# Reordering the columns of a normalized activation so that whole tiles can leave the meta columns out

## The reference, cut to what matters

```python
xn = rmsnorm(h, norm_mix)                       # 16 meta + 1024 prompt rows; 32 sample rows
z = xn @ w_in                                   # B, C, H (512 each), q, k, v (512 each), gate (512), a, beta
conv_out, new_a = causal_dwconv(z_C * z_H, buf_a, conv_a_w)      # 3 taps: reaches 2 rows back
y_a = z_B * conv_out
qkv, new_qkv = causal_dwconv(z_qkv, buf_qkv, conv_qkv_w)         # 4 taps
o, S = gated_delta_chunked(q, k, v, g, beta, state)              # recurrent over all rows, meta rows too
y_b = rmsnorm(o, gdn_norm) * silu(gate)
h = h + concat([y_a, y_b]) @ w_out
h = h + relu(rmsnorm(h) @ w_up)**2 @ w_down
y_prompt = rmsnorm(h, norm_final)[:, 16:]       # the meta rows are dropped
```

## Time and profile before

| | |
|---|---|
| Time, median of 3 runs | 1257.67 us (1257.44 to 1259.98) |
| Profiled execution, its own time | 1257.46 us |
| Its span, first to last instruction | 1255.7 us |
| PE busy | 1237.1 us (99%), 7950 matmuls |
| DVE, ACT, POOL busy | 801.7, 462.4, 646.7 us |
| PE idle from 0 to 43.33 us | 43.33 - 36.41 = 6.9 us |
| PE idle from 200 to 477 us | 277.00 - 276.21 = 0.8 us |
| granted PE clock, mean | 0.998 |

### The profile page before, as it was taken

How to read it: one execution, slowest core, us unless ns; L and a number is a source line. 1 busy time by engine, 2 the same in 40 slices (tenths; PEclk the granted TensorE clock), 3 DMA queues, 4 the chain that set the end, 5 groups by cost and what they waited for, 6 DMA issues and landing times.

```text
span 1255.7 us, 20503 instructions
## 1 busy us (share of the span) xinstructions
PE 1237.1 (99%) x7950; PEld 1090.9 (87%) x7950; DVE 801.7 (64%) x1283; ACT 462.4 (37%) x810; POOL 646.7 (52%) x503
## 2 busy tenths in 40 slices
PE   7999999999999999999999999999999999999997
PEld 6899999899999999998778888888887888878897
DVE  6465899535564766655987685565666667556456
ACT  6565654311222222224333333333434533333312
POOL 2332120112111212213889898888789989887811
PEclk9999999999999999999999999999999999999999
DMA  6132672843323322231145353444655442541003
GB/s 205 43 85 71 176 211 72 220 123 93 93 68 85 103 68 84 79 92 52 44 158 170 121 165 136 141 143 151 226 168 202 168 140 96 201 135 68 17 10 129
DMA packets 164706, 151.07 MB, mean 120 GB/s; under 512 B 21095, under 2 KB 141315, under 8 KB 161922
## 3 DMA queue, kind: packets, MB, share of 16 engines
q1 hardware_dynamic: 141634, 136.88, 34.4%
q10 hardware_dynamic: 22976, 12.88, 3.7%
HBM read 103.25 MB, written 46.49 MB: 119 GB/s over the span
## 4 chain that ended last, share of the span: by engine, by line
PE 95%; DVE 2%; POOL 1%; issue 1%; DMA 1%; ACT 1%; SPq 0%; POOLq 0%; DVEq 0%; ACTq 0%
PE banks L2328 15%; PE banks L2330 15%; PE banks L2331 15%; PE banks L1792 11%; PE banks L1794 11%; PE banks L1793 11%; PE banks L2359 1%; PE banks L2345 1%; PE banks L2441 1%; PE banks L2442 1%; PE banks L2443 1%; PE banks L2262 1%; PE banks L1978 1%; DMA w_raw<-in_w_in 1%; PE banks L1971 1%
## 5 line engine op out<-in xcount | busy, mean ns | idle before, releaser
L1792 PE MATMUL banks<-xn_high,w_high 128*128 128x384 f32 (+1 forms) x672 | 227.2, 338 | 1.0 <-DVE xn_low L2565 0.9
L1794 PE MATMUL banks<-xn_high,w_low 128*128 128x384 f32 (+1 forms) x672 | 218.9, 326 | 0.0
L1793 PE MATMUL banks<-xn_low,w_high 128*128 128x384 f32 (+1 forms) x672 | 218.8, 326 | 0.0
L1002 POOL TENSOR_TENSOR w_low<-w_raw,w_high 128x1024 fp32r<-128x1024 f32 x30 | 76.8, 2559 | 230.9 <-ACT w_high L1280 230.9
L3333 DVE TENSOR_TENSOR hT<-hT,banks 128x512 f32<-128x512 f32 x148 | 98.3, 684 | 109.2 <-PE banks L2331 108.4
L1792 PEld LDWEIGHTS banks<-xn_high,w_high 128*128 128x128 f32 x672 | 127.1, 189 | 6.8 <-issue 3.6
L2328 PE MATMUL banks<-op_high,set_high 128*128 128x512 f32 x336 | 131.6, 392 | 0.0
L2330 PE MATMUL banks<-op_low,set_high 128*128 128x512 f32 x336 | 130.8, 389 | 0.0
L2331 PE MATMUL banks<-op_high,set_low 128*128 128x512 f32 x336 | 130.7, 389 | 0.0
L1793 PEld LDWEIGHTS banks<-xn_low,w_high 128*128 128x128 f32 x672 | 127.4, 190 | 0.0
L1794 PEld LDWEIGHTS banks<-xn_high,w_low 128*128 128x128 f32 x672 | 127.0, 189 | 0.0
(11 more groups left out here) (419 smaller groups left out, 2839.9 us busy)
## 6 DMA issues: line engine op xcount, KB each, us to landing
op_raw<-ops_kept SPq DMA_DIRECT2D x21, 1024.0 KB, 5.0
w_up_raw<-in_w_up SPq DMA_DIRECT2D x16, 1024.0 KB, 6.5
w_raw<-in_w_in SPq DMA_DIRECT2D x28, 512.0 KB, 4.4
ops_kept<-u_rows SPq DMA_DIRECT2D x28, 512.0 KB, 2.7
ops_kept<-u_T SPq DMA_DIRECT2D x42, 256.0 KB, 2.4
w_down_half<-in_w_down SPq DMA_DIRECT2D x3, 2048.0 KB, 9.0
w_down<-in_w_down SPq DMA_DIRECT2D x24, 256.0 KB, 4.2
w_raw<-in_w_out SPq DMA_DIRECT2D x8, 512.0 KB, 3.8
```

Of the source, the lines that this page charges most:

```text
L1002: pool.tensor_tensor(w_l[n % 2][:, :, :], w_raw[n % 2][:, :, :], w_h[n % 2][:, :, :].bitcast(F32), ALU.subtract).then_inc(w_low, 1)
L1792: pe.matmul(bank[:, 0:w], w_h[n % 2][:, k, :], hi[:, c0:c0 + w], start=(k == first), stop=False)
L1793: pe.matmul(bank[:, 0:w], w_h[n % 2][:, k, :], lo[:, c0:c0 + w], start=False, stop=False)
L1794: ins = pe.matmul(bank[:, 0:w], w_l[n % 2][:, k, :], hi[:, c0:c0 + w], start=False, stop=(k == last))
```

## The change

The columns of the normalized x (`xn_high`, `xn_low`) are laid out as meta, prompt, samples; the groups become 272, 384 and 416 columns wide. Everything that is made from them (q, k, v, C, H, B, `abT`) keeps its old layout, so each eviction of the last group is split in a main piece and a piece of 32 sample columns, and the first group's is a single piece. Tiles of gate and B skip the first 16 columns of group 0 and tiles of C and H the first 14, in the matmuls and in the evictions. The gate's rows in DRAM have no meta columns any more. The samples of token tile 0 are transposed with group 2 instead of group 0, as a fourth piece of each k-slice. `idle_products` is written in terms of `GROUPS[0][1]`, so its width goes from 208 to 240 columns.

```diff
-GROUPS = [(0, C0 + 2 * P), (C0 + 2 * P, 3 * P), (C0 + 5 * P, 3 * P)]
+GROUPS = [(0, META + 2 * P), (META + 2 * P, 3 * P), (META + 5 * P, 3 * P + NS)]
...
-        gate_d = scratch("gate_kept_rows", [NH, P, TOK])
+        gate_d = scratch("gate_kept_rows", [NH, P, KEPT])
...
+        def unused(n, g):
+
+            return {"gate": META, "B": META, "C": META - 2, "H": META - 2}.get(IN_TILES[n][0], 0) if g == 0 else 0
+
+        def group_tiles(g):
+
+            pieces = [(0, slice(NS, C0))] if g == 0 else []
+            pieces += [(t, slice(0, P)) for t in GTILES[g] if t]
+            return pieces + ([(0, slice(0, NS))] if g == 2 else [])
+
+        def main_cols(g, skip=0):
+
+            c0, w = GROUPS[g]
+            w -= NS if g == 2 else 0
+            return slice(skip, w), slice(NS + c0 + skip, NS + c0 + w)
+
+        SAMPLE_COLS = slice(3 * P, 3 * P + NS)
+
+        def feature_cols(g, skip=0):
+
+            return [main_cols(g, skip)] + ([(SAMPLE_COLS, slice(0, NS))] if g == 2 else [])
+
+        def without_meta(cols):
+            return slice(cols.start - META, cols.stop - META) if cols.start >= C0 else cols
...
                     act.wait_ge(acc_done, 3 * n + g + 1)
-                    if g == 0:
+                    made, kept = main_cols(g)
+                    act.activation(zb[:, 59 - NS + kept.start:59 - NS + kept.stop], bank[:, made], ACT.Copy)
+                    if g == 2:
                         act.activation(zb[:, 0:56].rearrange("p (b r) -> p b r", r=7)[:, :, 3:7],
-                                       bank[:, 0:NS].rearrange("p (b r) -> p b r", r=LSEQ), ACT.Copy)
-                        act.activation(zb[:, 59:59 + w - NS], bank[:, NS:w], ACT.Copy)
-                    else:
-                        act.activation(zb[:, 59 + c0 - NS:59 + c0 - NS + w], bank[:, 0:w], ACT.Copy)
-                    act.activation(dst[:, c0:c0 + w], bank[:, 0:w], ACT.Copy, scale=now).then_inc(acc_read_act, 1)
+                                       bank[:, SAMPLE_COLS].rearrange("p (b r) -> p b r", r=LSEQ), ACT.Copy)
+                    for made, kept in parts:
+                        ins = act.activation(dst[:, kept], bank[:, made], ACT.Copy, scale=now)
+                    ins.then_inc(acc_read_act, 1)
...
-                    act.activation(z[0][:, c0:c0 + w], bank[:, 0:w], ACT.Copy).then_inc(acc_read_act, 1)
+                    for made, kept in parts:
+                        ins = act.activation(z[0][:, kept], bank[:, made], ACT.Copy)
+                    ins.then_inc(acc_read_act, 1)
...
                 act.wait_ge(acc_read_dve, dve_reads_to(n) + g + 1)
-                act.activation(ya_h[:, i, c0:c0 + w], z[1][:, c0:c0 + w], ACT.Copy).then_inc(ya_high_s, 1)
+                parts = feature_cols(g, unused(n, g))
+                for _, kept in parts:
+                    cols = without_meta(kept)
+                    ins = act.activation(ya_h[:, i, cols], z[1][:, cols], ACT.Copy)
+                ins.then_inc(ya_high_s, 1)
...
                 c0, w = (GROUPS if n < N_IN else KEPT_GROUPS)[g]
-                bank = in_bank(n, g) if n < N_IN else out_bank(n, g)
+                skip = unused(n, g) if n < N_IN else 0
+                bank = (in_bank(n, g) if n < N_IN else out_bank(n, g))[:, skip:w]
+                cols = slice(c0 + skip, c0 + w)
                 for k in ks:
                     hi, lo = rhs(k)
-                    pe.matmul(bank[:, 0:w], w_h[n % 2][:, k, :], hi[:, c0:c0 + w], start=(k == first), stop=False)
+                    pe.matmul(bank, w_h[n % 2][:, k, :], hi[:, cols], start=(k == first), stop=False)
...
                 g, k = m // KT, m % KT
-                c0 = GROUPS[g][0]
+                o = 0
                 pe.wait_ge(x_low, m - 4 if m >= KT + 5 else m - KT + 4)
-                for t in GTILES[g]:
-                    o, c = tile_cols(t)
+                for t, tokens in group_tiles(g):
+                    c = tokens.stop - tokens.start
                     if k == 0:
                         pe.wait_ge(x_scaled, t + 1)
-                    ins = pe.transpose(ps[turn_bank(g, k)][:, o - c0:o - c0 + c], x_tile(t)[:, P * k:P * k + P],
-                                       eye[0:c, 0:c])
+                    ins = pe.transpose(ps[turn_bank(g, k)][:, o:o + c], x_tile(t)[tokens, P * k:P * k + P],
+                                       eye[tokens, tokens])
+                    o += c
                 ins.then_inc(x_turned, 1)
```

More of the change, by code:

```diff
@@ L808, in step @@
                     sp.wait_ge(acc_read_act, 3 * n + 3)
-                    sp.dma_start(gate_d[h], gate[h % 2][:, :]).then_inc(gate_sent[h % 2], 16)
+                    sp.dma_start(gate_d[h], gate[h % 2][:, 0:KEPT]).then_inc(gate_sent[h % 2], 16)
                 if u == max(SOLVE):
@@ L1290, in keep_ab @@
             def keep_ab(g):
-                c0, w = GROUPS[g]
                 act.wait_ge(ab_made, g + 1)
-                act.activation(abT[:, c0:c0 + w], ps[7 - g % 2][0:16, 0:w], ACT.Copy).then_inc(ab_kept, 1)
+                for made, kept in feature_cols(g):
+                    ins = act.activation(abT[:, kept], ps[7 - g % 2][0:16, made], ACT.Copy)
+                ins.then_inc(ab_kept, 1)
             for t in GTILES[0]:
@@ L1388, in evict @@
                     act.wait_ge(acc_done, 3 * n + g + 1)
-                    act.activation(gate[i % 2][:, c0:c0 + w], bank[:, 0:w], ACT.Silu).then_inc(acc_read_act, 1)
+                    for made, kept in parts:
+                        ins = act.activation(gate[i % 2][:, without_meta(kept)], bank[:, made], ACT.Silu)
+                    ins.then_inc(acc_read_act, 1)
                 if kind == "C":
@@ L1788, in dense_part @@
                 c0, w = (GROUPS if n < N_IN else KEPT_GROUPS)[g]
-                bank = in_bank(n, g) if n < N_IN else out_bank(n, g)
+                skip = unused(n, g) if n < N_IN else 0
+                bank = (in_bank(n, g) if n < N_IN else out_bank(n, g))[:, skip:w]
+                cols = slice(c0 + skip, c0 + w)
                 for k in ks:
                     hi, lo = rhs(k)
-                    pe.matmul(bank[:, 0:w], w_h[n % 2][:, k, :], hi[:, c0:c0 + w], start=(k == first), stop=False)
-                    pe.matmul(bank[:, 0:w], w_h[n % 2][:, k, :], lo[:, c0:c0 + w], start=False, stop=False)
-                    ins = pe.matmul(bank[:, 0:w], w_l[n % 2][:, k, :], hi[:, c0:c0 + w], start=False, stop=(k == last))
+                    pe.matmul(bank, w_h[n % 2][:, k, :], hi[:, cols], start=(k == first), stop=False)
+                    pe.matmul(bank, w_h[n % 2][:, k, :], lo[:, cols], start=False, stop=False)
+                    ins = pe.matmul(bank, w_l[n % 2][:, k, :], hi[:, cols], start=False, stop=(k == last))
                     if k == last:
@@ L1828, in _ @@
                 pe.wait_ge(x_scaled, t + 1)
-                o, c = tile_cols(t)
+                o, tokens = (META + P * (t - 1), slice(0, P)) if t else (0, slice(NS, C0))
                 for k in range(KT):
-                    ins = pe.transpose(ps[turn_bank(0, k)][:, o:o + c], x_tile(t)[:, P * k:P * k + P], eye[0:c, 0:c])
+                    ins = pe.transpose(ps[turn_bank(0, k)][:, o:o + tokens.stop - tokens.start],
+                                       x_tile(t)[tokens, P * k:P * k + P], eye[tokens, tokens])
                     if t == GTILES[0][-1]:
```

34 lines of the change are left out of this document (14 added, 20 removed).

## The result

The changed kernel takes 1259.8 us (median of 20 runs, 1258.4 to 1262.6), the kernel before 1257.7 us in the same comparison (20 runs, 1255.5 to 1260.0). The ratio, estimated from all runs, is 1.0021, 95% interval 1.0015 to 1.0027. So the change makes the kernel slower, by 2.1 us between the medians (0.17%) and by 0.21% in the ratio. That is clear of noise, but the interval holds the bound of 0.2%, so which side of it the loss lies on isn't settled. The forecast was 1257.0 us, no difference, with a range up to 1259.5: it is wrong in the sign and, by 0.3 us, in the range. The profiled execution spans 1257.8 us, 2.1 more than before.

The account below looks back on a forecast made before the run. PE was taken to bound the kernel, busy 1237.1 of 1255.7 us. Columns -2.2, start +0.4 and give-backs +1.1 summed to -0.7 us, so 1257.67 became 1257.0 us, no difference, range 1255.0 to 1259.5.

Parts of the forecast that it names:

- Eight transposes more: At the start, one 32-column sample transpose per k-slice, priced 0.077 us each from twelve 28-column ones: +0.6 us.
- The bound above: Upper bound for the whole start, +0.8 us, with no waits absorbing and 0.38 us open; the estimate was +0.4.
- tightest slack: PE's `use_state` at 323.40 us, where DVE's `vn` is ready 0.77 us ahead; a shorter group 0 block takes 0.45.
- The columns: PE's shorter streams in gate, B, C and H tiles, less group 2's wider ones: -2.2 us, bounds -2.0 to -2.4.
- Rival 3: C and H blocks of group 0 start unaligned at column 14 and might step slower, up to +23 us; 4%.
- The second price: Skill's figure for streams of weight load and matmul, 0.13 ns a column, making the cut 0.75 us; not used.
- The give-backs: PE waits growing at two `turn_o`, ACT's extra copy and the stage's end: 0.47 + 0.45 + 0.1 + 0.1 = +1.1 us.
- Rivals 1 and 2: DVE-POOL collisions before PE waits: gone, 1255.2 us, 14%; or new, one 1258.7 us, 9%, two 1260.4 us, 5%.
- The products without use: At the start, 32 more columns in six records: +0.38 us on PE, all but 0.04 covered by the wait behind.
- The slow steps: At the start, seventeen or so matmuls at PE's slower clock, with a step of 0.227 us in the changed profile.
- 0.02 us a tile: In k, q and v tiles, 32 columns moving from group 0 to group 2 change nothing, within this amount.
- Rival 4: Last group's k, q, v evictions end 0.2 us later and hold up DVE: +2.4 us, 1259.4 us; 6%.

Follow-up runs that it names:

- row32: Kernel before, with eight added 32-row transposes in a row behind the last k-slice of group 2, output unread; ratio 1.0000 (0.9985 to 1.0014).
- pairs32: Kernel before, with eight added unread 32-row transposes, two in a row in every second k-slice of group 2; ratio 1.0012 (0.9999 to 1.0025).
- whole: Changed kernel, with each sample piece transposed as a full 128-row tile, rows filled by a 320 KB load; ratio 1.0010 (0.9996 to 1.0023).
- fullstream: Changed kernel, with PE again streaming the unused columns of group 0, written and never read; ratio 1.0042 (1.0030 to 1.0055).
- idle208: Changed kernel, with the six products without use at their old width of 208 columns; ratio 1.0028 (1.0014 to 1.0043).
- after_again: Changed kernel run once more without an edit, on the chip of the run fullstream; ratio 1.0028 (1.0017 to 1.0038).
- piece32: Kernel before, with one more 32-row transpose in each k-slice of group 2, to unread bank columns; ratio 1.0006 (0.9994 to 1.0018).
- piece128: Kernel before, with one more full 128-row transpose in each k-slice of group 2, to unread bank columns; ratio 1.0012 (0.9999 to 1.0026).
- metafirst: Kernel before, columns ordered meta, samples, prompt, old groups, no added transposes, unused group 0 columns skipped; ratios 0.9988 and, repeated, 0.9991.

## Why the prediction was wrong, step by step

**The step that failed** is "Eight transposes more": "I take 8 x 0.077 = +0.6 us". The term was there, and its size was off: it measured 2.68 us, 0.335 each on the mean (seven at 0.37, and one in the place of a wait of 0.30 us for `xn_low`, as the prediction said that part might). The prediction has no word on the change of height. The row behind the 0.077 has twelve transposes of 28 rows behind each other, in which the change of height occurs once. The new ones stand each alone between products of 128 rows, which pays for it eight times. row32, with the rows' own arrangement, measured 0.83 us; pairs32 and whole lie where the number of changes puts them. The bound above, +0.8 for the whole start, was made from the same row and so could not hold it. With 2.68 in place of 0.6 the sum is -0.7 + 2.1 = +1.4 us.

**The unpredicted wait** is another 0.4 us: the prediction's tightest slack was 0.77 us at `use_state`, and there was a tighter one, in a transfer. ACT issues the loads of `At` and `X` at 291.56 us, one block ahead of PE's first use. The timelines of ACT and PE in the changed kernel:

```profile
292.01 0.58 ACTq L1454 DMA_DIRECT2D X<-X_kept  x1
```

```profile
297.74 0.44 PE L2060 MATMUL banks<-X,At 32*32 32x32 f32 x16 [0.26 <-issue]
```

The row names nothing, but L2060 waits for the two loads and for little else, and the row of the DMA issues between 285 and 300 us gives the time from issue to landing:

```profile
X<-X_kept ACTq DMA_DIRECT2D x1, 256.0 KB, 5.6
```

292.01 + 5.6 is 297.6, and PE starts at 297.74. Before, the same load landed 5.2 us after its issue at 290.47, about 0.25 us ahead of PE's use at 295.92. The load took longer, and the time left for it was nearly the same: from the issue to the use there were 5.45 us before, and 5.74 here with 0.33 of delay, or 5.41 without. A wait of this kind of over 0.2 us is in six of the other traces too, between 0.25 and 0.56 us, and one of them is pairs32, whose blocks are as wide as before:

```profile
384.98 0.44 PE L2026 MATMUL banks<-X,At 32*32 32x32 f32 x16 [0.56 <-issue]
```

That load was issued at 378.90 us and landed after 6.0, at 384.9. So the landing ends the wait, and shorter blocks are not needed for it. Why the load takes longer in some traces isn't known. In the changed kernel two steps of PE ahead of L2060 are longer than before: that of 297.74 by 0.33 us and that of 386.19, where the load landed 5.5 us after its issue at 380.64, by 0.10, which no idle time shows.

**The columns** were right: between the bounds of -2.0 and -2.4 us, the blocks measured -2.06. The timeline of PE has steps of 256, 258 and 416 columns:

```profile
305.46 0.28 PE L1828 MATMUL banks<-xn_high,w_high 128*128 128x256 f32 x1
...
307.84 0.28 PE L1830 MATMUL banks<-xn_high,w_low 128*128 128x256 f32 x1
...
340.45 0.28 PE L1828 MATMUL banks<-xn_high,w_high 128*128 128x258 f32 x1
...
342.85 0.28 PE L1830 MATMUL banks<-xn_high,w_low 128*128 128x258 f32 x1
```

Twenty steps take 2.38 us (0.119) and 2.40 us (0.120). 416 columns took 0.189 (22 steps from 298.41 to 302.56), against 0.187 to 0.188. The two prices per column differ by so little that a gate or B tile saves 0.14 us and a C or H tile 0.11. Rival 3, the stream that starts at column 14, is out: 258 columns step within 0.001 us of 256. The second price of the Trainium skill (TensorE: Matmul & The Clock Gate, "Back-to-back issue gap"), weighed and not used, doesn't fit here: by 0.13 ns a column the 8 x 24 x (16 + 14) = 5,760 columns would be 0.75 us, and fullstream, which puts these columns back, lost 2.0 without its additional wait.

**The give-backs** were right to 0.05 us. The timeline of PE after, beside the earlier trace rows:

```profile
314.53 0.66 PE L2124 MATMUL banks<-c_main,o_tok 128*128 128x128 f32 x4 [1.02 <-DVE o_tok L2975]
...
343.96 0.66 PE L2124 MATMUL banks<-c_main,o_tok 128*128 128x128 f32 x4 [0.82 <-DVE o_tok L2975]
...
483.07 0.40 PE L1828 MATMUL banks<-ya_high,w_high 128*128 128x288 f32 x1 [0.60 <-DVE ya_low L2801]
```

They grew by 0.50 (0.47 expected), 0.54 (0.55) and 0.11 (0.1). Rivals 1 and 2 did not happen. At 340 us, DVE and POOL in the changed kernel still collide in the same order, beside the earlier trace rows:

```profile
340.90 2.27 DVE L2974 TENSOR_TENSOR fo<-fo,rq_s 128x4 f32<-128x4 f32 x1
```

```profile
340.76 2.39 POOL L1027 TENSOR_TENSOR w_low<-w_raw,w_high 128x1024 fp32r<-128x1024 f32 x1 [2.37 <-ACT w_high L1305]
```

POOL starts 0.14 us ahead where it was 0.22. In the stage that makes -2.06 of columns, +1.15 of these waits and +0.43 of the load, or -0.48; measured is -0.41, and the rest is spread over the other steps.

**The start but for the transposes** was right in kind. The products without use cost 0.24 us more and not 0.38: they take 7.71 - 5.00 = 2.71 us where they took 7.84 - 5.37 = 2.47. The slow steps came at 0.227 us (14 steps from 13.77 to 16.95 us, at 272 columns, PE's lower clock of 1.2 GHz), and the idle products went into the wait (idle208). In the k, q and v tiles the shift of 32 columns to group 2 cost 0.20 us in eleven tiles, 0.018 each, within the "0.02 us a tile" that the prediction gave and left out of the sum. Rival 4 would be +2.4 us in that stretch and is out.

Together: -0.7 as predicted, +2.1 transposes, +0.4 the load, +0.2 the tiles make +2.0 us, where +2.1 was measured. That the sum closes so well is in part luck of the two executions: the stretch ahead of the start alone was 1.3 us shorter in after_again.

## What to carry to other kernels

Take a duration from a row that has the same neighbours, not only the same shape: twelve small transposes in a row say little about one small transpose between full ones. Before a layout splits a tile into pieces of another height, count the changes of height that PE's queue gets, and see if the pieces can stand in a row or be padded to full height; here a layout without the split kept the gain in columns. And when you list the slacks, list the transfers too, not only the engines: this one landed 0.25 us ahead of its use before, and it took 4.9 to 5.9 us to land in the thirteen traces.

## What the runs showed of the hardware

- One change between weight loads of 128 and 32 rows and back cost 0.31 us on PE, at 0.17 us of idle time in the row of the loads, while PE's own row shows no wait (piece32, pairs32, row32). A full transpose in the same place cost 0.11 us (piece128), a lone small one 0.37.
- The moment at which PE's clock goes from 1.2 to 2.4 GHz at the start differs between executions: the steps at 272 or 304 columns fall by nearly half at 17.69 us in the trace before, at 14.43 in metafirst and with the first product in after_again (13.33). With 15 steps of 0.253 us and not 0.140, as before, it is worth up to 1.7 us of the span, and I take it for a good part of the scatter of the times. The granted clock in the windows of those microseconds reads 1.00 in all of them; only the steps show it.
- Five of thirteen traces have one further fall in block u=6, behind 18 products of 8 columns that took 2.1 us in all of them. The windows of row32 (PE, PEld, DVE, ACT, POOL, then the granted clock):

```profile
54.00:58.70 4.70, 4.70 (x36) 4.41 (x35) 0.60 (x5) 2.62 (x4) 1.63 (x6) 1.00 0.37 104
58.70:62.20 3.50, 3.50 (x17) 3.50 (x16) 3.15 (x6) 2.77 (x3) 0.83 (x4) 0.51 0.04 11
62.20:66.00 3.80, 3.80 (x25) 3.80 (x25) 3.76 (x4) 2.67 (x8) 2.40 (x1) 1.00 0.50 143
```

Here the granted clock does show it, 0.51, with 17 products where the kernel before had 25. It costs 1.5 us: 155.9 to 156.1 us from u=3 to u=36 in piece32, row32, fullstream, idle208 and the second run of metafirst, 154.4 to 154.6 in the others. What decides whether it falls isn't known; no experiment varied it.
